# Two transformer-like blocks on one core: projection and logits by token tile, first experts gathered in pairs

## What is computed

```python
def first_block(x, ...):
    hn = rmsnorm(h, attn_norm_g)
    q, k, v, u, vg = split(hn @ w_in)
    mixed = concatenate([rmsnorm(stick_breaking_attention(q, k, v)), rmsnorm(gating(u, vg))])
    h = h + mixed @ w_out                       # 1024 x 1024, "out1" below
    hn = rmsnorm(h, ffn_norm_g)
    h = h + hierarchical_moe(hn, ...)
    return rmsnorm(h, final_norm_g)

def hierarchical_moe(xt, ...):                  # 4 groups of 8 experts, D_EXPERT 512
    g_logits = xt @ w_router_group + b          # best group
    e_logits = (xt @ w_router_expert)[group] + b   # its two best experts, renormalised
    for each expert e: h = silu(xt @ w_gate[e]) * (xt @ w_up[e]);  out += (h * combine[:, e]) @ w_down[e]
```

## Time and profile before

| | us |
|---|---|
| median of 3 runs | 1065.51 (1065.05 to 1067.79) |
| the profiled execution, its own time | 1067.41 |
| its span in the profile | 1065.7 |
| TensorE, products busy | 884.1 (83%) |
| VectorE busy | 534.2 (50%) |
| ScalarE busy | 348.3 (33%) |
| DMA, mean over the span | 282 GB/s |

### The profile page before, as it was taken

How to read it: one execution, slowest core, us unless ns; L and a number is a source line. 1 busy time by engine, 2 the same in 40 slices (tenths; PEclk the granted TensorE clock), 3 DMA queues, 4 the chain that set the end, 5 groups by cost and what they waited for, 6 DMA issues and landing times.

```text
span 1065.7 us, 18042 instructions
## 1 busy us (share of the span) xinstructions
PE 884.1 (83%) x7875; PEld 714.9 (67%) x7875; DVE 534.2 (50%) x854; ACT 348.3 (33%) x467; POOL 114.2 (11%) x55
## 2 busy tenths in 40 slices
PE   8998998775574757464666899999999989999997
PEld 8988965442232424242423699589999989989985
DVE  4546464132031312121121999999997857544542
ACT  4654211100000000010001644476656445533531
POOL 1030000000000000000010498505110000000000
PEclk9998989987687878687788999999999999999999
DMA  9850689999999999999999655244567544446421
GB/s 342 258 235 2 282 340 429 425 426 428 426 429 428 428 429 428 430 426 430 426 429 413 201 175 182 80 132 150 192 221 254 202 168 167 177 167 225 161 79 40
DMA packets 86888, 299.99 MB, mean 282 GB/s; under 512 B 12541, under 2 KB 50861, under 8 KB 74413
## 3 DMA queue, kind: packets, MB, share of 16 engines
q1 hardware_dynamic: 86685, 299.13, 71.6%
q10 hardware_dynamic: 144, 0.00, 0.0%
HBM read 298.07 MB, written 1.05 MB: 281 GB/s over the span
## 4 chain that ended last, share of the span: by engine, by line
PE 54%; DMA 29%; DVE 13%; issue 2%; ACT 1%; SPq 1%; DVEq 0%; ACTq 0%
DMA mem<-in_w_up 25%; PE PS L1811 12%; PE PS L1812 12%; PE PS L1813 12%; PE PS L2011 8%; DVE PS L1583 6%; PE PS L2024 3%; DMA mem<-in_w_down 2%; PE PS L1785 1%; DVE PS L1608 1%; DVE X L1615 1%; DMA mem<-in_w 1%; DMA mem<-in_w_in 1%; PE PS L1997 1%; SPq L501 1%
## 5 line engine op out<-in xcount | busy, mean ns | idle before, releaser
L2011 PE MATMUL PS<-mem 128*32 128x256 f32 x2048 | 155.1, 470 | 141.1 <-DMA mem<-in_w_up 140.6
L2011 PEld LDWEIGHTS PS<-mem 128*32 128x32 f32 x2048 | 80.7, 135 | 216.9 <-issue 147.5
L1813 PE MATMUL PS<-HT_hi,ring_rest 128*128 128x256 f32 x744 | 211.0, 284 | 0.0
L1358 DVE TENSOR_TENSOR mem<-mem,PS 128x128 f32<-128x128 f32 x32 | 12.1, 380 | 265.1 <-ACT mem L825 265.1
L1813 PEld LDWEIGHTS PS<-HT_hi,ring_rest 128*128 128x128 f32 x744 | 143.0, 192 | 0.0
L1811 PE MATMUL PS<-HT_hi,z_hi 128*128 128x256 f32 x432 | 123.3, 285 | 2.5 <-DVE ring_rest L1558 2.5
L1812 PE MATMUL PS<-HT_rest,z_hi 128*128 128x256 f32 x432 | 122.9, 284 | 0.0
L1724 DVE TENSOR_TENSOR ring_rest<-mem,mlp_hi 128x4096 fp32r<-128x4096 f32 x16 | 70.8, 4424 | 57.8 <-ACT mlp_hi L1043 57.8
L825 ACT ACTIVATE mem<-PS 128x128 f32<-128x128 f32 x32 | 8.9, 278 | 276.3 <-PE PS L2011 276.3
L655 POOL TENSOR_TENSOR ring_rest<-mem,z_hi 128x2048 fp32r<-128x2048 f32 x19 | 88.5, 4672 | 88.0 <-DVE ring_rest L1558 51.4
L1583 DVE SCALAR_TENSOR_TENSOR PS<-mem,CAW,PS 128x256 f32<-128x256 f32 x232 | 91.3, 489 | 0.0
(11 more groups left out here) (365 smaller groups left out, 1796.9 us busy)
## 6 DMA issues: line engine op xcount, KB each, us to landing
mem<-in_w_gate SPq DMA_DIRECT2D x32, 2048.0 KB, 16.6
mem<-in_w_up SPq DMA_DIRECT2D x32, 2048.0 KB, 21.1
mem<-in_w_down SPq DMA_DIRECT2D x31, 2048.0 KB, 13.1
mem<-in_w SPq DMA_DIRECT2D x16, 2048.0 KB, 8.0
mem<-in_w_in SPq DMA_DIRECT2D x30, 1024.0 KB, 5.3
mem<-in_w_in SPq DMA_DIRECT2D x4, 2048.0 KB, 18.5
mem<-in_w_b_out SPq DMA_DIRECT2D x4, 1536.0 KB, 8.8
mem<-in_w_out SPq DMA_DIRECT2D x4, 1024.0 KB, 11.9
```

Of the source, the lines that this page charges most:

```text
L1358: nc.vector.tensor_tensor(by_row(hid[:, i % 2, :]), silu[:, i % 2, :].rearrange("p (m k) -> p m k", k=STRIPS), PS[:, B_GATE + i % 2, P:2 * ...
L1813: ins = nc.tensor.matmul(dst, s_rest, m_hi, start=False, stop=stop and n == len(terms) - 1, skip_group_check=True)
L2011: ins = nc.tensor.matmul(PS[SLOTS * j:SLOTS * (j + 1), bank, 0:2 * F_STRIP].rearrange("p (w n) -> p w n", w=2), xg[:, k, :], w[:, :, k, F_ ...
```

## The change

It has five parts.

- SyncE loads expert 2's matrices when the gated rows are scaled (`rows` at 4) and the last attention product is done (`av_done` at 4), and no longer waits for all mixed rows.
- The last products of the projection go by token tile: n = 2 and 3 of tile 0, n = 2 of tile 1, then tile 0's transposes, n = 3 of tile 1, tile 0's logits, tile 1's transposes and tile 1's logits. ScalarE sums each tile's squares as its `x_ready` comes, and VectorE applies the gain to tile 0 between its last two adds. The logits wait for each half of a tile, not for the tile.
- VectorE scales tile 0's rows before the logits and tile 1's behind the routing; the weights' five small operations go behind the selection.
- Four products without use in place of five.
- The first pack is gathered for experts 0 and 1 (`gather_two(0)`, all eight chunks with 64 columns, one bank, one eviction `take_two(0)`), and for experts 2 and 3 behind expert 0's gate and up (`turn_weights`, `gather_two(1)`), with the eviction behind `plan_extra_tiles`.

```diff
@@ SyncE
-            sp.wait_ge(rows, rows_before["ffn"])
+            sp.wait_ge(rows, rows_before["mix"] + TT)
+            sp.wait_ge(av_done, PAIRS)
             sp.wait_ge(tables_turned, 1)
             load_gate_up(THIRD_EXPERT, third)
@@ ScalarE
-            act.wait_ge(x_ready, 4)
-            row_squares("ffn", 8)
+            for tt in range(TT):
+                act.wait_ge(x_ready, 3 + tt)
+                add_squares(X[:, tt, :], 8 + tt, square)
+            rms("ffn", 8, TT, D)
@@ VectorE
-            for n in range(4):
-                dve.wait_ge(out1_ps, rows_done(n // 2, n % 2))
+            for n, done_count in enumerate((3, 4, 6, 8)):
+                dve.wait_ge(out1_ps, done_count)
...
+                if n >= 2:
+                    apply_gain("ffn", G_FFN, range(2 * (n - 2), 2 * (n - 2) + 2))
...
+            inverse_rms("ffn", 8, TT)
             dve.wait_ge(x_ready, 4)
-            normalise("ffn", 8)
+            normal_rows(0)
...
+            normal_rows(1)
+            dve.wait_ge(rank_ps, 1)
...
+            link(ins)
+            dve.sem_inc(sel_ready, 1)
             dve.wait_ge(r_exp, 1)
...
-            take_gathered(0)
+            def take_two(r):
+                dve.wait_ge(gath_ps, r + 1)
+                nc.vector.tensor_tensor(XG[:, :, 2 * SLOTS * r:2 * SLOTS * (r + 1)],
+                                        PS[:, (B_GATHER, B_SECOND)[r], :].rearrange("p (k s) -> p k s", k=KC),
+                                        gains[:, G_FFN, :].unsqueeze(2).broadcast_to((P, KC, 2 * SLOTS)), ALU.mult).then_inc(xg_ready, 1)
+
+            take_two(0)
...
                     plan_extra_tiles()
+                    take_two(1)
@@ TensorE
-            for n in range(4):
-                out1_product(n, 0)
-
-            turn_x((x_ready, 3), (x_ready, 4))
...
+            for n in range(2):
+                out1_product(n, 0)
+            out1_product(2, 0, (0,))
+            out1_product(3, 0, (0,))
+            out1_product(2, 0, (1,))
+            turn_x_tile(0, x_ready, 3)
+            out1_product(3, 0, (1,))
+            pe.wait_ge(router_loaded, 16 * N_ROUTER)
+            router_logits(0)
+            turn_x_tile(1, x_ready, 4)
+            router_logits(1).then_inc(logits_ps, 1)
+
+            keep_busy(3, 4)
...
+            def gather_two(r):
+                slots = slice(2 * SLOTS * r, 2 * SLOTS * (r + 1))
+                for k in range(KC):
+                    for tt in range(TT):
+                        ins = nc.tensor.matmul(PS[:, (B_GATHER, B_SECOND)[r], 2 * SLOTS * k:2 * SLOTS * (k + 1)], HN[:, tt, k, :],
+                                               sel[:, tt, slots], start=tt == 0, stop=tt == TT - 1)
+                ins.then_inc(gath_ps, 1)
...
-            gather(0)
+            pe.wait_ge(sel_ready, 1)
+            gather_two(0)
...
                 expert_gate_up(pack, 0)
+                if isinstance(pack, int):
+                    pe.wait_ge(sel_ready, 2)
+                    turn_weights()
+                    gather_two(1)
```

More of the change, by code:

```diff
@@ L1328, in _ @@
             dve.sem_inc(sel_ready, 1)
+            dve.wait_ge(r_exp, 1)
+            w1c, w2c = r_a[:, :, 8:9], r_a[:, :, 9:10]
+            link(nc.vector.tensor_reduce(r_a[:, :, 6:7], r_a[:, :, 0:GROUPS], AX_X, ALU.add))
+            link(nc.vector.tensor_scalar(r_a[:, :, 7:8], r_a[:, :, GROUPS:GROUPS + 1], 1.0, None, ALU.add))
+            link(nc.vector.tensor_tensor(r_a[:, :, 6:7], r_a[:, :, 6:7], r_a[:, :, 7:8], ALU.mult))
+            link(nc.vector.reciprocal(w1c, r_a[:, :, 6:7]))
+            link(nc.vector.tensor_tensor(w2c, w1c, r_a[:, :, GROUPS:GROUPS + 1], ALU.mult))
             link(nc.vector.tensor_tensor(hot1, hot1, over(w1c, EXPERTS_PER_GROUP), ALU.mult))
@@ L1795, in turn_rows, with turn_x_tile @@
                     ins.then_inc(turned, 1)
-            def turn_x(*ready):
-                for n in range(4):
-                    tt, half = n // 2, n % 2
-                    if n % 2 == 0:
-                        pe.wait_ge(*ready[tt])
+            def turn_x_tile(tt, ready, count):
+                pe.wait_ge(ready, count)
+                for n in (2 * tt, 2 * tt + 1):
+                    half = n % 2
                     for k in range(4):
@@ L1938, in turn_mix, with out1_product @@
                     ins.then_inc(turned, 1)
-            def out1_product(n, half):
+            def out1_product(n, half, tiles=range(TT)):
                 pe.wait_ge(out1_rest_ready, OUT1_SPLIT.index(n) + 1)
-                for tt in range(TT):
+                for tt in tiles:
                     terms = rows_times(tt, out1_hi[n][:, :, :], out1_half(n)[1])[KC // 2 * half:KC // 2 * (half + 1)]
@@ L1966, in _, with router_logits @@
             pe.wait_ge(hT_rest_ready, split_count("mix", 2 * TT - 1))
-            for n in range(4):
-                out1_product(n, 0)
-            turn_x((x_ready, 3), (x_ready, 4))
-            pe.wait_ge(router_loaded, 16 * N_ROUTER)
-            for tt in range(TT):
+            def router_logits(tt):
                 at = tt * (GROUPS + EXPERTS)
-                pe.wait_ge(hT_ready, hT_count("ffn", 2 * tt + 1))
                 for k in range(KC):
+                    if k % 4 == 0:
+                        pe.wait_ge(hT_ready, hT_count("ffn", 2 * tt + k // 4))
                     ins = nc.tensor.matmul(PS[:, 0, at:at + GROUPS + EXPERTS], HT[:, k, tt * P:(tt + 1) * P], w_router[:, k, :],
                                            start=k == 0, stop=k == KC - 1)
-            ins.then_inc(logits_ps, 1)
-            keep_busy(3, 5)
+                return ins
+            for n in range(2):
[10 more added lines that the diff above has]
+            keep_busy(3, 4)
             pe.wait_ge(routed_ready, TT)
@@ L1989, in gather @@
             def gather(pack):
-                pe.wait_ge(sel_ready, pack + (1 if isinstance(pack, int) and pack == 0 else 2))
+                pe.wait_ge(sel_ready, pack + 2)
                 pe.wait_ge(ct_ready, pack)
@@ L2000, in gather, with turn_weights @@
                 pe.wait_ge(xg_ready, 2 * pack + 1)
-                if isinstance(pack, int) and pack == 0:
-                    pe.wait_ge(sel_ready, 2)
+                turn_weights()
+            def gather_two(r):
+                slots = slice(2 * SLOTS * r, 2 * SLOTS * (r + 1))
+                for k in range(KC):
+                    for tt in range(TT):
+                        ins = nc.tensor.matmul(PS[:, (B_GATHER, B_SECOND)[r], 2 * SLOTS * k:2 * SLOTS * (k + 1)], HN[:, tt, k, :],
+                                               sel[:, tt, slots], start=tt == 0, stop=tt == TT - 1)
+                ins.then_inc(gath_ps, 1)
+            def turn_weights():
                 for tt in range(TT):
@@ L2054, in expert_gate_up @@
             def expert_gate_up(pack, i):
-                if i == 0:
+                if isinstance(pack, int) and pack == 0:
+                    pe.wait_ge(xg_ready, i // 2 + 1)
+                elif i == 0:
                     pe.wait_ge(xg_ready, 2 * pack + 2)
```

18 lines of the change are left out of this document (4 added, 14 removed).

## The result

The changed kernel takes 1070.70 us in the median (1068.78 to 1073.25, five runs), the kernel before 1065.51 on the same chip. The ratio is 1.0044, with a 95% interval of 1.0029 to 1.0058: slower by some 5 us, where 1064.8 and a range of 1062.0 to 1067.8 had been forecast. The prediction was wrong in its sign and in its range.

A forecast was written before the change was run, and what follows sets the result against it. The kernel waits for the experts' weights over DMA, a stream held by gu_done 1. Ranks 0.75 and gather 0.05 gained, hole 0.1 lost: 0.7 us, so the median goes from 1065.5 to 1064.8, range 1062.0 to 1067.8.

The forecast's parts named there:

- The rule: The time changes by what moves gu_done 1, the first expert's gate and up products, and by nothing else before it.
- SyncE's waits: The third expert's loads are issued 4.9 us earlier, when nothing wants them: worth 0 us.
- Order by tile: Last projection products, transposes and logits by token tile: logits' end between 0.3 us gained and 0.2 lost.
- Keep-busy: Four products without use instead of five between logits and ranks: rank result 0.35 us earlier if the clock falls.
- ranks: Tile 1's rows scaled in the wait for the ranks on VectorE: 1.2 us gained in the good case.
- Gather by its stationary side: First gather's pitch is set by 128 stationary columns; 64 moving columns gain 0.0 to 0.3 us, 0.05 taken.
- both cases occur: Clock's fall and return ahead of the ranks differ between runs: 0.35 us gained or 1.2, 0.75 taken.
- rival 1: First gather goes by its moving columns, its 64-column products half as long: 1.9 us more gained, 1062.9; chance 0.07.
- Rival 3: Clock falls in the first gather; with gate and up low too, 4.6 us less 0.7, 1069.4, slower; chance 0.12.
- Second gather: With turned weights, 4.1 us before expert 1's gate/up; expert 3's down load lands in time by 0.6; 0.1 lost.

The follow-up runs named there:

- after: The changed kernel with all five parts of the change, against the kernel before: 1070.70 us, ratio 1.0044.
- the pair with the clock held: Six products without use ahead of the ranks, more behind: changed kernel (two more) 0.9995; changed kernel with one gather of four (one more) 0.9993.

## Why the prediction was wrong, point by point

- **The rule** (the time changes by what gu_done 1 moves) held in direction: the four profiles with a stage over 31.8 us belong to the four highest medians. It isn't exact: stages 1.6 shorter left the median alone, and equal code differs by 0.7 between gu_done 1 and the last combine.
- **SyncE's waits, 0 us:** right. Alone 0.9993; the load went out 15.28 us ahead of the second add, and in after the DMA moved 7 GB/s between 146 and 156 us.
- **Order by tile, 0.3 gained to 0.2 lost:** right for the change as a whole, since the logits end 11.67 behind the second add (134.97), a little before the forecast 11.8 to 12.3. Against the old order with the clock also high (11.52) that is 0.15 lost. What I hadn't priced is the order without the moved rows, 0.9 us or 1.0017.
- **Keep-busy 0.35 and ranks up to 1.2, 0.75 taken: the first step that failed.** It was worked out from a trace in which the clock fell in the logits, and set the whole move forward against it. The move did happen: the gather starts 1.8 us sooner behind the second add than in that trace. But it starts there without the change too, each time the clock holds through the logits (19.04 with SyncE's waits alone, 19.07 with four products, 19.24 in after), and then the low clock is paid for in the gather. Against the second way the gain is 0. I had written that "both cases occur" and still sized the gain on one.
- **Gather by its stationary side, 0.05 gained:** right at full clock (3.68 for 64 columns, 3.84 for 128, 3.76 for 32), and rival 1 is out. As a term of the sum it failed, since the sum let the narrow gather run at full clock: with the fall it came to 2.82 us lost up to gu_done 1.
- **Rival 3, the clock falls in the gather, chance 0.12: the second step that failed, and the one that decided.** Its mechanism was right, and its size in the sum: 4.6 us for gather and gate and up all low, measured 12.79 - 8.18 = 4.6. In this there is some luck, for the parts came out the other way round: 1.9 and 2.7 had been worked out for gather and gate and up, 2.7 (6.36 less 3.68) and 1.9 (5.57 less 3.66) were measured. Its 1069.4 is 1.3 below the median. The chance was wrong. The fall in the gather or in the ranks just ahead of it is not rare: it came in 9 of the 11 profiled executions without added products behind the ranks, in all those where the clock had not fallen in the logits; and with the order by tile it fell in the logits in none of eight. My argument against it, the 32-column products of the earlier trace rows at full clock, proved nothing: they ran inside a busy stretch with the clock already high, whereas the question was whether narrow products bring a low clock back.
- **Second gather, 0.1 lost:** not settled. The means of the traces give 0.6, with ranges that overlap, the pair with the clock held about 0, and the median of the run with the second one alone 1.5, part of it the clock's. The load did come late by what was forecast (9.20 for 9.3); whether its slack was used up no row shows.
- **Range:** its upper end took rival 3 with the gather alone low and left out the rival's own 1069.4, with gate and up low too. The measured 1070.70 lies above both.

## What to carry to other kernels

Look in the windows at the granted clock of every short stage on the path, in more than one execution: a stage may pass in two ways at the same price, and a gain worked out on one of them need not be one on the other. Before narrowing a product, ask not what it costs at full clock but whether the clock may fall just ahead of it; a few wide products, even without use, in the wait ahead of it kept the narrow form harmless here (1065.80 against 1070.70). A piece of work moved off the path, as the second gather, still has to be checked against the loads that wait behind it; here they came 4 us later, at a price between 0 and 0.6 us.

## What the runs showed of the hardware

- After a fall at the same place the way back differs with the width of what runs. Falls 19 to 21 us behind the second add: about 3 us at 0.50 with 128-column products in the gather (four executions), about 10 with 64-column ones (three). Falls 17.5 us behind it: 6.4 with 128 columns, 13 with 64 (one each). With 64 columns the low clock lasted through gate and up as well.
- At full clock 32 fp32 records with 128 stationary columns take 3.76, 3.68 and 3.84 us for 32, 64 and 128 moving columns: the narrow form saves at most 0.16 us.
- Where the low clock falls isn't set by the code alone: the kernel before had it in the logits in two profiles; with SyncE's waits alone changed, and with four products in place of five (an edit behind the logits), it was in the gather. The stages differ by 0.4 us at most.
